# Gates of a hybrid encoder layer by the exponential and VectorE's reciprocal, in place of ScalarE's sigmoid and silu

## Chip, cores and metric

The kernel runs on 1 core of one Trainium2 chip. The metric is the device time of one launch in microseconds. Three runs of the kernel before gave 1577.31 to 1579.09 us, median 1578.4.

## The reference, cut to what matters

One layer over 272 tokens (16 learned ones and 256 of the input), width 2048, float32: RMSNorm, one input projection, a convolution group and a gated DeltaNet group side by side, one output projection, a residual, then RMSNorm and a mixture of 32 experts. The gates that the change touches are these:

```
u = rmsnorm(h, attn_norm[l])
glu_a, glu_b, qkv, z, beta_logit, decay_logit = split_in_proj(u @ w_in[l])
# conformer_conv
y = glu_a * jax.nn.sigmoid(glu_b)
y = causal_depthwise_conv(y, w_dw) + b_dw          # 31 taps
...
# gated_deltanet
qkv = jax.nn.silu(causal_depthwise_conv(qkv, sc_w))   # 4 taps
...
o = chunk_gated_delta_rule(q, k, v, beta, g)
o = o * lax.rsqrt(jnp.mean(o * o, axis=-1, keepdims=True) + EPS) * norm_g
o = o * jax.nn.silu(z)
```

## The kernel before

The input projection makes 48 tiles of 128 output columns by 272 tokens (256 for z), one after the other, in two PSUM banks by turns: bank `n % 2` for tile n. `TILES` fixes their order by kind: "b" and "a" are the halves of the convolution's gate, "c" the 24 tiles of q, k and v, "z" the 8 tiles of the output gate. The order is b b a a b b a a (tiles 0 to 7), 12 c (8 to 19), b b a a (20 to 23), 12 c (24 to 35), b b a a (36 to 39), 8 z (40 to 47). TensorE makes each tile in four quarters (`project`, L704). Before it starts tile n it waits until tile n-2 has been read from the bank (`tile_read0`, `tile_read1`).

Each engine has its instructions in a fixed order written out by hand. Between the quarters TensorE makes steps of the delta rule (`delta`): six groups, one for each half of the heads and each chunk of tokens (one chunk of 16, two of 128). The steps of a group are "turn" (transposes), "decay", "lvl0" (L750 and the lines behind it), then pairs a and b of a triangular solve (L773 and L790, L793; L769 and L786 for the last), "solve" (L799), "apply" (L808, L810), "back" (L817). `STEP_SLOTS` says behind which quarter a step comes. ScalarE, VectorE and GpSimd make their parts of a step in the same order, each between its own work on tiles. ScalarE's part has Ln and Exp for the norms (L1249 to L1258, L1281, L1283) and copies of the solve's products (L1266, L1268, L1271). VectorE's part of "lvl0" is L1568 to L1575, of the solve L1582 to L1590. GpSimd makes the masks (L1996).

ScalarE's work on a tile of kind b is a sigmoid from the bank into `gate_e`, of kind z a silu from the bank into `gate_e` (both in L1295); that read frees the bank. `gate_e` has two halves, used by turns. For a c tile it copies the bank to `raw` (L1206), which frees the bank; VectorE convolves (L1529, L1531), and ScalarE applies silu to the tile before (L1211). ScalarE's functions lie in table sets: `use_table` loads a set (L1160) only when the name differs from the last one, and its calls stand ahead of the waits. VectorE's work on an a tile is one product of bank and gate (L1663), which frees the bank; on a z tile two products or copies of `gate_e` into `mixT` (L1674, L1676), and the bank is long free. All VectorE's gaps are filled with the taps of the 31-tap convolution (L1635), two behind each quarter once the delta steps run.

After tile 47 the output projection (L852) takes banks 0 and 1 first: it waits until both have been read 24 times, then for the last "back" step. Layer norm, router, gather and experts follow. SyncE issues all weight loads; those of the experts wait for slots that the output projection frees (L542), and later for the experts' own products.

Of the kernel before, what the change touches and what calls it, by code (L numbers as in the profile page):

```python
# [207 lines left out]
def hybrid_kernel(nc, x, meta, attn_norm, w_in, conv_dw_w, conv_dw_b, conv_ln_g, conv_ln_b, short_conv_w,  # L208
                  a_log, dt_bias, delta_norm_g, w_out, ffn_norm, w_group, b_group, w_router, b_router,
                  w_gate, w_up, w_down, final_norm, cst_in, masks_in, out):  # L210
    with ExitStack() as ctx:
# [3 lines left out]
        def sem(name):  # L215
            return ctx.enter_context(nc.semaphore(name))
# [158 lines left out]
        tile_read1 = sem("tile_read1")  # L375
        short_done = sem("short_done")
        silu_done = sem("silu_done")
        gated = sem("gated")
        conv_tap = sem("conv_tap")
        delta_pe = sem("delta_pe")  # L380
# [769 lines left out]
        def _(act):  # L1150
            act_fn = nc.scalar.activation
            own = Order(act, order_act)

            table = ""

            def use_table(name):

                nonlocal table
                if name != table:
                    act.preload_act_table_set(name)  # L1160
                table = name

            def ln_exp_table():
                use_table("natural_log_exp_and_others")
            ln_exp_table()

            def rstd_of(i, m):
# [45 lines left out]

            def gate_logits():

                ln_exp_table()
                act.wait_ge(gate_dve, 2)
                act_fn(tb[:, :, :], ta[:, :, :], ACT.Exp, scale=-1.0).then_inc(gate_act, 1)
                act_fn(beta[:, :, :], ba_tok[:, :, 0:NH], ACT.Exp, scale=-1.0).then_inc(gate_act, 1)
                act.wait_ge(later_loaded, 16 * N_LATER)  # L1220
                act_fn(ea, alog_b[:, :], ACT.Exp).then_inc(gate_act, 1)
                act.wait_ge(gate_act, 1)
                act_fn(ta[:, :, :], tb[:, :, :], ACT.Ln, bias=1.0).then_inc(gate_act, 1)

            def decays():

                ln_exp_table()
                act.wait_ge(gsum_done, 1)
                for c, (_, m) in enumerate(CHUNKS):
                    for at, n_ in ((0, m), (8, m), (16, P)):  # L1230
                        act_fn(egs[0:n_, c, at:at + 8], banks[6][0:n_, 24 * c + at:24 * c + at + 8], ACT.Exp
                               ).then_inc(gexp_ready, 1)

            def delta():
                for g in GROUPS:
                    c, hh = g
                    t0, m = CHUNKS[c]
                    act.wait_ge(delta_pe, PE_AT[(g, "turn")])
                    act_fn(k_tok[0:m], bk[2][0:m], ACT.Copy)
                    act_fn(r_tok[0:m], bk[3][0:m], ACT.Copy)  # L1240
                    last = act_fn(scratch[0:m], bk[2][0:m], ACT.Square)
                    if c:
                        last = act_fn(x_inv[0:m], bk[4][0:m], ACT.Square)
                    last.then_inc(delta_act, 1)
                    yield

                    ln_exp_table()
                    act.wait_ge(delta_dve, DVE_AT[(g, "turn")])
                    own.then(act_fn(lnt[0:m], kk[0:m], ACT.Ln, bias=EPS))  # L1249
                    if c:  # L1250
                        own.then(act_fn(lnq[0:m], qq[0:m], ACT.Ln, bias=EPS))
                    own.settle()
                    own.then(act_fn(rk[0:m], lnt[0:m], ACT.Exp, scale=-0.5))
                    if c:
                        own.then(act_fn(rq[0:m], lnq[0:m], ACT.Exp, scale=-0.5))
                        own.then(act_fn(rq2[0:m], lnq[0:m], ACT.Exp, scale=-1.0))
                    act.wait_ge(delta_pe, PE_AT[(g, "decay")])
                    act_fn(decay[0:m, :, 0:m], bk[6][0:m, :, 0:m], ACT.Exp).then_inc(delta_act, 1)  # L1258
                    if c:
                        act_fn(att[0:m, :, 0:m], bk[7][0:m, :, 0:m], ACT.Exp).then_inc(delta_act, 1)  # L1260
                    yield
                    yield
                    for v in range(1, n_levels(c)):
                        act.wait_ge(delta_pe, PE_AT[(g, f"a{v}")])
                        if c == 0:
                            last = act_fn(scratch[0:m, :, 0:m], bk[3][0:m, :, 0:m], ACT.Copy)  # L1266
                        elif v == JOIN:
                            last = act_fn(scratch[0:CAP, :, CAP:P], bk[3][0:CAP, :, CAP:P], ACT.Copy)  # L1268
                        else:
                            for b_, lo in zip(A_BANKS, HALVES):  # L1270
                                last = act_fn(scratch[lo, :, lo], bk[b_][lo, :, lo], ACT.Copy)  # L1271
                        last.then_inc(delta_act, 1)
                        yield
                        yield
                    act.wait_ge(delta_pe, PE_AT[(g, "solve")])
                    act_fn(w_tok[0:m], bk[7][0:m], ACT.Copy).then_inc(delta_act, 1)
                    yield
                    if c:
                        ln_exp_table()
                        act.wait_ge(delta_dve, DVE_AT[(g, "apply")])  # L1280
                        own.then(act_fn(lnt[0:m], oo[0:m], ACT.Ln, bias=EPS))  # L1281
                        own.settle()
                        act_fn(ro[0:m], lnt[0:m], ACT.Exp, scale=-0.5).then_inc(delta_act, 1)  # L1283
                    yield
                    if c:
                        yield

            def gate(n, kind, m):

                use_table("silu_and_others" if kind == "z" else "sigmoid_and_others")  # L1290
                act.wait_ge(tile_done, n + 1)
                if m >= 2:
                    act.wait_ge(gated, m - 1)
                width = SEQ if kind == "z" else T
                return act_fn(gate_e[:, T * (m % 2):T * (m % 2) + width], banks[n % 2][:, 0:width],  # L1295
                              ACT.Silu if kind == "z" else ACT.Sigmoid)

            steps = delta()
            i_c = m_gate = 0
            for n, (kind, j, _, _) in enumerate(TILES):  # L1300
                for _ in range(sum(STEP_SLOTS[n])):
                    next(steps, None)
                if kind == "c":
                    use_table("silu_and_others")
                    take_raw(n, i_c)

                    if i_c % (QKV // 2) > 0:
                        silu_raw(i_c - 1)
                    if n in LAST_C:
                        silu_raw(i_c)  # L1310
                    i_c += 1
                elif kind in "bz":

                    gate(n, kind, m_gate).then_inc((tile_read0, tile_read1)[n % 2], 1)
                    m_gate += 1
                if n == 12:
                    gate_logits()
                if n == 15:
                    decays()
# [1 line left out]
                pass  # L1321


            ln_exp_table()
            for i in range(4):
                act.wait_ge(ln_dve, i + 1)
                act_fn(ln_sq[i], mixT[:, 2 * i:2 * i + 2, :], ACT.Square).then_inc(ln_act, 1)
            for i in range(4):
# [2 lines left out]
                                scale=1.0 / P))  # L1331
                own.settle()
                act_fn(ln_sq[i], ln_sq[i], ACT.Exp, scale=-0.5).then_inc(ln_act, 1)
            use_table("silu_and_others")
            for i in range(4):
                act.wait_ge(ln_dve, 5 + i)
                act_fn(mixT[:, 2 * i:2 * i + 2, :], mixT[:, 2 * i:2 * i + 2, :], ACT.Silu).then_inc(mix_done, 1)  # L1337
# [75 lines left out]
                pair(r * PAIRS + PAIRS - 1, True)  # L1413


            use_table("silu_and_others")
            act.wait_ge(plan_ready, 1)
            silu(0, 0)
            pair(0, False)
# [31 lines left out]
        def _(dve):  # L1451
# [3 lines left out]
            def step(ins):  # L1455

                own.then(ins)
                own.settle()
# [195 lines left out]
            def gate(n, kind, j, m):  # L1654

                nonlocal n_gated, n_silu_z
                width = SEQ if kind == "z" else T
                e = gate_e[:, T * (m % 2):T * (m % 2) + width]
                if kind == "a":

                    dve.wait_ge((tile_read0, tile_read1)[n % 2], n // 2)
                    dve.wait_ge(tile_done, n + 1)
                    step(tt(glu[:, j, HISTORY:], banks[n % 2][:, 0:T], e, ALU.mult))  # L1663
                    n_gated = j + 1
                    dve.sem_inc((tile_read0, tile_read1)[n % 2], 1)
                else:
                    dve.wait_ge((tile_read0, tile_read1)[n % 2], n // 2 + 1)
                    for c in (1, 2):
                        v, ec = mixT[:, 8 + j, P * (c - 1):P * c], e[:, P * (c - 1):P * c]
                        g = (c, j // 4)  # L1670
                        if g in back_done:

                            dve.wait_ge(delta_dve, DVE_AT[(g, "back")])
                            own.then(tt(v, v, ec, ALU.mult))  # L1674
                        else:
                            own.then(dve.tensor_copy(v, ec))  # L1676
                    own.settle()
                    n_silu_z += 1

                dve.sem_inc(gated, 1)  # L1680

            steps = delta()
# [354 lines left out]
```

## Time and profile before

| | us |
|---|---|
| median of 3 runs | 1578.4 |
| the profiled execution, its own time | 1579.09 |
| its span, first to last instruction | 1577.3 |
| TensorE busy | 1540.8 |
| VectorE busy | 524.0 |
| ScalarE busy | 229.9 |
| of it 36 table loads | 46.2 |
| mean granted TensorE clock | 0.994 |

The span is what the trace covers; the time of the execution holds some 2 us more. Busy time of an engine is no measure of its limit: waits are read from the lists of waits and the timelines.

### The profile page before, as it was taken

How to read it: one execution, taken by the hardware profiler on the slowest of the kernel's cores; microseconds unless marked ns; L12 is line 12 of the kernel's file. 1: busy time of each engine (PE TensorE's matmuls, PEld its weight loads, DVE VectorE, ACT ScalarE, POOL GpSimd, SP SyncE). 2: the span in 40 equal slices, each digit the busy share in tenths (PEclk: the TensorE clock that was granted, in tenths of full speed). 3: DMA queues.
4: the chain of work that ended last, by engine and by line, in shares of the span. 5: the costliest groups of instructions: out<-in, count | busy, mean ns of one | idle time of the engine just before them, and what ended most of it. 6: DMA issues, size and time to landing. Idle time of an engine off the chain costs nothing.

```text
span 1577.3 us, 19577 instructions
## 1 busy us (share of the span) xinstructions
PE 1540.8 (98%) x8083; PEld 842.0 (53%) x8083; DVE 524.0 (33%) x1110; ACT 229.9 (15%) x481; POOL 52.9 (3%) x57
## 2 busy tenths in 40 slices
PE   8999999999999999999999999999999999999997
PEld 6878777777776445444344344344434434434432
DVE  2466237843484213222221221321221321321323
ACT  2002223132221303100000100100000000000003
POOL 0000021102020000000000000000000000000000
PEclk9999999999999999999999999999999999999999
DMA  9634231232234126899999999999999999999995
GB/s 346 201 128 168 107 108 38 71 107 107 108 108 189 77 107 267 354 371 429 427 429 428 429 428 428 429 428 429 428 430 428 429 428 429 429 428 430 427 429 201
DMA packets 69575, 479.50 MB, mean 304 GB/s; under 512 B 11506, under 2 KB 20227, under 8 KB 41987
## 3 DMA queue, kind: packets, MB, share of 16 engines
q1 hardware_dynamic: 69232, 478.55, 74.0%
q8 instruction: 37, 0.61, 0.2%
q10 hardware_dynamic: 290, 0.23, 0.1%
q14 instruction: 16, 0.12, 0.0%
HBM read 476.66 MB, written 2.10 MB: 304 GB/s over the span
## 4 chain that ended last, share of the span: by engine, by line
PE 71%; DMA 22%; DVE 4%; SPq 1%; issue 1%; ACT 1%; ACTq 0%; POOL 0%; DVEq 0%
DMA ring<-in_w_up_dram 21%; PE bank L704 20%; PE bank L1030 18%; PE bank L1053 9%; PE bank L1100 7%; PE bank L852 7%; PE bank L995 1%; DVE region_m L1635 1%; PE bank L790 1%; PE bank L1046 1%; PE bank L773 1%; SPq L568 1%; PE bank L793 0%; PE bank L667 0%; DMA rows<-in_conv_ln_b_dram 0%
## 5 line engine op out<-in xcount | busy, mean ns | idle before, releaser
L1030 PE MATMUL bank<-ring,region_m 128*64 128x512 f32 x2048 | 456.3, 596 | 7.9 <-DMA ring<-in_w_up_dram 7.9
L704 PE MATMUL bank<-region_u,ring 128*128 128x272 f32 (+1 forms) x1536 | 373.8, 396 | 0.0
L704 PEld LDWEIGHTS bank<-region_u,ring 128*128 128x128 f32 x1536 | 284.6, 190 | 55.1 <-issue 0.9
L1030 PEld LDWEIGHTS bank<-ring,region_m 128*64 128x64 f32 x2048 | 141.6, 137 | 283.5 <-issue 261.8
L1053 PE MATMUL bank<-region_qy,region_s 128*64 128x512 f32 x992 | 218.2, 592 | 0.5 <-issue 0.5
L1053 PEld LDWEIGHTS bank<-region_qy,region_s 128*64 128x64 f32 x992 | 72.2, 137 | 140.7 <-issue 140.4
L1869 DVE TENSOR_TENSOR region_s<-region_s,bank 64x512 f32<-64x512 f32 x32 | 22.1, 692 | 348.4 <-ACT region_s L1378 348.4
L995 PEld LDWEIGHTS bank<-region_m,region_u 128*128 128x128 f32 x960 | 108.4, 192 | 12.2 <-issue 12.2
L1100 PE MATMUL bank<-region_m 128*128 128x512 f32 x256 | 114.8, 600 | 0.0
L1885 DVE TENSOR_TENSOR region_h<-region_h,bank 128x512 f32<-128x512 f32 x128 | 88.0, 688 | 79.1 <-PE bank L1100 79.1
L1635 DVE SCALAR_TENSOR_TENSOR region_m<-region_qy,cols,region_m 128x256 f32<-128x256 f32 x240 | 110.6, 525 | 2.1 <-DVE region_qy L1663 1.0
L995 PE MATMUL bank<-region_m,region_u 128*128 128x128 f32 x960 | 111.2, 277 | 0.0
L1879 DVE COPY region_m<-bank 64x512 f32<-64x512 f32 x64 | 44.1, 689 | 169.8 <-PE bank L1053 169.3
L852 PE MATMUL bank<-ring,region_m 128*128 128x512 f32 x192 | 85.0, 595 | 0.8 <-ACT region_m L1337 0.8
L1100 PEld LDWEIGHTS bank<-region_m 128*128 128x128 f32 x256 | 46.9, 190 | 67.6 <-issue 63.7
L1383 ACT ACTIVATE region_s<-bank 128x256 f32<-128x256 f32 x32 | 12.3, 384 | 431.8 <-PE bank L1046 431.7
L1396 ACT ACTIVATE region_m<-bank 64x512 f32<-64x512 f32 x64 | 37.9, 592 | 195.9 <-PE bank L1053 195.5
L1861 DVE TENSOR_TENSOR region_m<-bank,g_ffn_pm 128x512 f32<-128x512 f32 x64 | 44.1, 692 | 56.9 <-PE bank L995 56.7
L852 PEld LDWEIGHTS bank<-ring,region_m 128*128 128x128 f32 x192 | 35.8, 190 | 43.5 <-issue 43.4
L1378 ACT ACTIVATE region_s<-bank 64x512 f32<-64x512 f32 x32 | 18.9, 589 | 226.2 <-PE bank L1030 226.2
L1160 ACT ACT_TABLE_LOAD x36 | 46.2, 1283 | 1.4 <-PEq L2026 0.8
L2011 POOL TENSOR_TENSOR region_u<-region_h,ring 128x512 f32<-128x512 f32 x2 | 3.0, 1496 | 1093.2 <-DVE region_h L1885 1093.2
(263 smaller groups left out, 843.8 us busy)
## 6 DMA issues: line engine op xcount, KB each, us to landing
ring<-in_w_gate_dram SPq DMA_DIRECT2D x63, 2048.0 KB, 12.2
ring<-in_w_up_dram SPq DMA_DIRECT2D x63, 2048.0 KB, 16.7
region_qy<-in_w_down_dram SPq DMA_DIRECT2D x62, 2048.0 KB, 15.6
ring<-in_w_in_dram SPq DMA_DIRECT2D x40, 1024.0 KB, 7.4
ring<-in_w_out_dram SPq DMA_DIRECT2D x12, 1024.0 KB, 5.5
ring<-in_w_in_dram SPq DMA_DIRECT2D x16, 512.0 KB, 5.4
region_qy<-in_w_out_dram SPq DMA_DIRECT2D x4, 1024.0 KB, 13.1
ring<-in_w_down_dram SPq DMA_DIRECT2D x2, 2048.0 KB, 26.4
```

Of the source, the lines that this page charges most:

```text
L704: last = mm(banks[n % 2][:, 0:width], slot[s][:, 512 * k + P * j:512 * k + P * (j + 1)], uT[:, 4 * g + k, T - width:T], start=g == k == 0, ...
L852: last = mm(banks[4 * t + q], mixT[:, k, P * t:P * (t + 1)], w_slots[n_k][:, BANK * q:BANK * (q + 1)], start=n_k == 0, stop=n_k == KD - 1)
L995: last = mm(banks[5 + g % 2][:, P * k:P * (k + 1)], un[:, t, c0:c0 + P], sel_g[:, t, :], start=t == 0, stop=t == TT - 1)
L1030: last = mm(banks[x_][CAP * v:CAP * (v + 1), :], uTe[:, 4 * g + k, CAP * x_:CAP * (x_ + 1)], w_gu[v][:, k0:k0 + 512], start=g == k == 0, s ...
L1053: last = mm(banks[3 + q][CAP * v:CAP * (v + 1), :], hidT[:, x_, f, :], w[f // 2][:, c0:c0 + BANK], start=n_f == 0, stop=n_f == KF - 1)
L1100: mm(banks[sb[i % len(sb)]], sel_wT[:, P * (i // 4):P * (i // 4 + 1)], ypair[:, column(i)], start=True, stop=True).then_inc(scatter_done, 1)
L1160: act.preload_act_table_set(name)
L1396: last = act_fn(ypair[CAP * x_:CAP * (x_ + 1), c0:c0 + BANK], banks[4][CAP * v:CAP * (v + 1), :], ACT.Copy)
L1635: stt(out=acc, in0=glu[:, j, tap:tap + SEQ], scalar=dw_w[:, tap, j:j + 1], in1=acc if tap else cols[:, 33 + j:34 + j].to_broadcast([P, SEQ ...
L1861: tt(uTe[:, 4 * g:4 * g + 4, :], bk[GATHER_FIRST[g] if isinstance(p, int) and p == 0 else 5 + g % 2], b4(g_ffn_pm[:, 4 * g:4 * g + 4]), AL ...
L1879: last = dve.tensor_copy(ypair[CAP * x_:CAP * (x_ + 1), c0:c0 + BANK], banks[3][CAP * v:CAP * (v + 1), :])
L1885: tt(v, v, banks[sb[i % len(sb)]][:, :], ALU.add).then_inc(scatter_read, 1)
```

## The change

ScalarE makes `exp(-x)` of every b and z tile. VectorE adds 1 and takes the reciprocal. For an a tile it then multiplies with the bank as before. For a z tile it multiplies the bank with the result, so that the silu is made, and then does what it did before. The signal that a z bank has been read moves from ScalarE to the end of VectorE's work, and a new semaphore `gate_exp` tells VectorE that the exponential is there. In `gate` the two instructions on an a tile stand behind both waits, that for the tile of the gate's other half too. Exp and Ln share one table set. `use_table` goes: `ln_exp_table` now always loads the log/exp set, and is called at the start, behind the silus of a c tile, and ahead of the second norm and the last one. No line loads the silu set any more; the compiler places a load of it before a silu where it isn't there. In the part before layer norm, ScalarE's order is otherwise the same.

```
-            def use_table(name):
-                nonlocal table
-                if name != table:
-                    act.preload_act_table_set(name)
-                table = name
...
             def ln_exp_table():
-                use_table("natural_log_exp_and_others")
+
+                act.preload_act_table_set("natural_log_exp_and_others")
...
             def gate(n, kind, m):
-                use_table("silu_and_others" if kind == "z" else "sigmoid_and_others")
                 act.wait_ge(tile_done, n + 1)
...
-                return act_fn(gate_e[:, T * (m % 2):T * (m % 2) + width], banks[n % 2][:, 0:width],
-                              ACT.Silu if kind == "z" else ACT.Sigmoid)
+                return act_fn(gate_e[:, T * (m % 2):T * (m % 2) + width], banks[n % 2][:, 0:width], ACT.Exp, scale=-1.0)
...
                 if kind == "c":
-                    use_table("silu_and_others")
                     take_raw(n, i_c)
 
                     if i_c % (QKV // 2) > 0:
                         silu_raw(i_c - 1)
                     if n in LAST_C:
                         silu_raw(i_c)
+                    if i_c % (QKV // 2) > 0:
+                        ln_exp_table()
                     i_c += 1
-                elif kind in "bz":
+                elif kind == "z":
+                    gate(n, kind, m_gate).then_inc(gate_exp, 1)
+                    m_gate += 1
+                elif kind == "b":
...
# VectorE
                 e = gate_e[:, T * (m % 2):T * (m % 2) + width]
-                if kind == "a":
+                if kind == "z":
+                    dve.wait_ge(gate_exp, j + 1)
+                else:
 
                     dve.wait_ge((tile_read0, tile_read1)[n % 2], n // 2)
                     dve.wait_ge(tile_done, n + 1)
+                step(ts(e, e, 1.0, None, ALU.add))
+                step(dve.reciprocal(e, e))
+                if kind == "a":
                     step(tt(glu[:, j, HISTORY:], banks[n % 2][:, 0:T], e, ALU.mult))
                     n_gated = j + 1
-                    dve.sem_inc((tile_read0, tile_read1)[n % 2], 1)
                 else:
-                    dve.wait_ge((tile_read0, tile_read1)[n % 2], n // 2 + 1)
+                    step(tt(e, banks[n % 2][:, 0:SEQ], e, ALU.mult))
                     for c in (1, 2):
...
                     n_silu_z += 1
 
+                dve.sem_inc((tile_read0, tile_read1)[n % 2], 1)
                 dve.sem_inc(gated, 1)
```

The calls of `ln_exp_table` in `gate_logits`, `decays`, in the delta steps and before the layer norm's Square go, and the two calls of `use_table("silu_and_others")` before the layer norm's silu and before the experts.

## Rows read from the trace of the kernel before

**Rows 1.** The page: busy time with instructions, and the chain's shares by engine.
```profile
PE 1540.8 (98%) x8083; PEld 842.0 (53%) x8083; DVE 524.0 (33%) x1110; ACT 229.9 (15%) x481; POOL 52.9 (3%) x57
...
PE 71%; DMA 22%; DVE 4%; SPq 1%; issue 1%; ACT 1%; ACTq 0%; POOL 0%; DVEq 0%
```
**Rows 2.** Waits of TensorE, 40 to 620 us: total, times, longest.
```profile
PE bank L773 <- DVE region_h L1575: 5.8, 4, 3.1
PE bank L817 <- DVE region_h L1607: 2.2, 4, 1.0
```
**Rows 3.** Groups by line: busy us and mean ns; idle time before them.
```profile
L1160 ACT ACT_TABLE_LOAD x36 | 46.2, 1283 | 1.4 <-PEq L2026 0.8
...
L1529 DVE TENSOR_SCALAR region_m<-region_qy,cols 128x272 f32<-128x272 f32 x24 | 8.7, 361 | 19.2 <-ACT region_qy L1206 19.2
L1663 DVE TENSOR_TENSOR region_qy<-bank,region_m 128x272 f32<-128x272 f32 x8 | 3.5, 442 | 38.2 <-PE bank L704 38.1
L1765 DVE RECIPROCAL small<-small 128x1 f32<-128x1 f32 x2 | 0.3, 164 | 0.1
L1519 DVE RECIPROCAL small<-small 128x24 f32<-128x24 f32 x1 | 0.3, 302 | 0.0
```
**Rows 4.** Timelines of ScalarE, GpSimd, TensorE, first short group: start, length, [idle].
```profile
166.32 1.28 ACT L1160 ACT_TABLE_LOAD   x1
167.61 0.20 ACT L1249 ACTIVATE small<-small 16x4 f32<-16x4 f32 x1
...
168.98 0.31 POOL L1996 TENSOR_TENSOR region_s<-region_h,masks 16x64 f32<-16x64 f32 x1 [2.68 <-DVE region_h L1561]
...
169.63 0.26 PE L750 MATMUL bank<-cst,region_s 16*16 16x16 f32 x4
```
**Rows 5.** Timeline of ScalarE behind a c tile.
```profile
309.71 0.38 ACT L1268 ACTIVATE region_h<-bank 64x256 f32<-64x256 f32 x1 [2.99 <-PE bank L769]
```
**Rows 6.** Timeline of VectorE from tile 42 to the layer norm.
```profile
448.95 0.48 DVE L1674 TENSOR_TENSOR region_m<-region_m 128x128 f32<-128x128 f32 x2
449.58 0.69 DVE L1568 TENSOR_TENSOR region_h<-cst,bank 128x512 f32<-128x512 f32 x1 [0.15 <-DVE region_m L1674]
...
463.31 0.85 DVE L1588 TENSOR_TENSOR region_h<-region_h,bank 64x256 f32<-64x256 f32 x2 [0.45 <-PE bank L793]
464.18 0.85 DVE L1590 TENSOR_TENSOR region_h<-region_h,bank 64x256 f32<-64x256 f32 x2
...
474.49 0.85 DVE L1588 TENSOR_TENSOR region_h<-region_h,bank 64x256 f32<-64x256 f32 x2 [1.05 <-PE bank L793]
...
485.13 0.41 DVE L1585 TENSOR_TENSOR region_h<-region_h,bank 64x256 f32<-64x256 f32 x1 [1.59 <-PE bank L786]
...
498.91 0.49 DVE L1674 TENSOR_TENSOR region_m<-region_m 128x128 f32<-128x128 f32 x2
513.08 0.69 DVE L1713 SCALAR_TENSOR_TENSOR region_m<-bank,region_m 128x512 f32<-128x512 f32 x1 [13.68 <-PE bank L915]
```
**Rows 7.** Timeline of TensorE in the z tiles.
```profile
453.55 0.68 PE L773 MATMUL bank<-region_h,region_m 64*64 64x64 f32 x16 [2.07 <-DVE region_h L1575]
...
465.17 0.68 PE L773 MATMUL bank<-region_h,region_m 64*64 64x64 f32 x16
...
486.85 1.05 PE L799 MATMUL bank<-region_h 128*128 128x128 f32 x8
...
498.29 13.90 PE L852 MATMUL bank<-ring,region_m 128*128 128x512 f32 x32
```
**Rows 8.** Timeline of TensorE behind the longest wait.
```profile
278.81 3.53 PE L704 MATMUL bank<-region_u,ring 128*128 128x272 f32 x8
...
283.55 2.10 PE L704 MATMUL bank<-region_u,ring 128*128 128x272 f32 x8
```
**Rows 9.** Busy time by stretch, each engine; then granted clock, DMA share, GB/s.
```profile
280.00:282.40 2.40, 2.40 (x8) 1.35 (x8) 2.40 (x4) 0.02 (x1) 0.99 (x1) 0.50 0.36 117
...
440.00:480.00 40.00, 37.20 (x368) 30.06 (x366) 32.38 (x62) 7.69 (x17) 10.60 (x8) 1.00 0.31 107
```

More of the change, by code:

```diff
@@ L377, in hybrid_kernel @@
         silu_done = sem("silu_done")
+        gate_exp = sem("gate_exp")
         gated = sem("gated")
@@ L1152, in _ @@
             own = Order(act, order_act)
-            table = ""
-            def use_table(name):
-                nonlocal table
-                if name != table:
-                    act.preload_act_table_set(name)
-                table = name
             def ln_exp_table():
-                use_table("natural_log_exp_and_others")
+                act.preload_act_table_set("natural_log_exp_and_others")
             ln_exp_table()
@@ L1214, in gate_logits @@
             def gate_logits():
-                ln_exp_table()
                 act.wait_ge(gate_dve, 2)
@@ L1225, in decays @@
             def decays():
-                ln_exp_table()
                 act.wait_ge(gsum_done, 1)
@@ L1245, in delta @@
                     yield
-                    ln_exp_table()
                     act.wait_ge(delta_dve, DVE_AT[(g, "turn")])
@@ L1278, in delta @@
                     if c:
-                        ln_exp_table()
                         act.wait_ge(delta_dve, DVE_AT[(g, "apply")])
@@ L1321, in _ @@
                 pass
-            ln_exp_table()
             for i in range(4):
@@ L1333, in _ @@
                 act_fn(ln_sq[i], ln_sq[i], ACT.Exp, scale=-0.5).then_inc(ln_act, 1)
-            use_table("silu_and_others")
             for i in range(4):
@@ L1413, in one_round @@
                 pair(r * PAIRS + PAIRS - 1, True)
-            use_table("silu_and_others")
             act.wait_ge(plan_ready, 1)
```

## The prediction

> **What bounds the kernel now.** I read the page first: TensorE is busy for 1540.8 of 1577.3 us, and the chain that ended last is 71% TensorE and 22% DMA [rows 1]. So the time moves only where TensorE comes to wait, or where the expert weights start to stream later. The change touches the mixer (up to tile 47, about 498 us). The first expert loads wait for slots that the output projection frees (L542 in SyncE's order, L852 in TensorE's). These loads have no other anchor, so a microsecond that TensorE loses before 498 us delays the output projection, then the weight stream, then the end: I carry it over one to one.
>
> Next the waits of TensorE over the mixer. The largest is L773 behind VectorE's L1575, 5.8 us in 4 times [rows 2]: the first product of the triangular solve waits for VectorE. None of its waits in the recurrence is put down to ScalarE. ScalarE's 36 table loads take 46.2 us [rows 3], but beside a TensorE that doesn't wait for them. Then I read the timelines of all engines where the recurrence runs beside the projections.
>
> **The change, part by part.** *Gates on ScalarE.* The sigmoid of 8 tiles and the silu of 8 become 16 exponentials of the same shapes: no change in length. Their table loads go. Where they were, TensorE waited for VectorE or for nothing, so I take 0 for this gain. Its bounds are 0 and 2.2 us, the wait at L817, whose release passes through ScalarE [rows 2].
>
> *Table loads at the 22 silus of convolved tiles.* Silu is not in the log/exp set, so each of the 22 needs one load ahead of it, and the new line loads the log/exp set behind it. That puts two loads between the copy of a tile (L1206) and ScalarE's next step of the recurrence. A load takes 1283 ns [rows 3], and in the timeline the next instruction starts some 0.02 us behind it, so the two take 2.6 us and the lost overlap of copy and silu 0.1: 2.7 us. The tightest place at 128 tokens is L1268, where ScalarE had been idle for 2.99 us [rows 5]: it still fits. (The Trainium skill, "ScalarE: Activation LUTs", What ACT_TABLE_LOAD costs, gives about 2.66 us for every switch, 1.38 of it a drain. This trace doesn't agree: the load before the Ln of [rows 4] starts at 166.32 and the Ln at 167.61, 1.29 us apart. By the page the pair would take 5.3 us, not 2.6.)
>
> It does not fit in the first group of each half, of 16 tokens. There the order of ScalarE before is silu, load, Ln; after, load, silu, load, Ln. The Ln (L1249) starts at 167.61, right behind its load; with one more load ahead, it starts 1.3 to 1.4 us later. GpSimd's mask at 168.98 hangs on it through VectorE and ends at 169.29; TensorE's L750 starts at 169.63 [rows 4]. So TensorE waits 169.29 + 1.4 - 169.63 = 1.1 us, and again in the second half (the same rows come again 177 us later): **+2.2 us**. Bounds: 0 and 2.8.
>
> *Gates on VectorE.* Each "a" tile gets an add of 1 and a reciprocal, each "z" tile these and one product that reads the bank. The add: the scaling of L1529, 128x272, takes 361 ns [rows 3]; I take 0.36. The product: L1663 takes 442 ns [rows 3]; for 256 columns 0.42. The reciprocal has no row of this size. The two that there are take 164 ns for one column and 302 ns for 24 [rows 3], 6.0 ns a column, so 164 + 255 x 6.0 = 1694 ns for 256. Lower bound: the rate of the product, 0.42. Upper: all of the 302 ns by column, 12.6 ns each, 3.2 us. I take 1.69, since it is the slope of the operation itself. With three settles of about 0.04 us, **D = 2.6 us** more for each z gate (1.3 to 4.1), and 2.2 for each a gate. (The Trainium skill, "VectorE: DVE Perf Modes", First, the fixed hardware budget, says that a reciprocal repeats its divide step 8 times. Taken as 8 cycles of 0.96 GHz, 8.3 ns a column, it would make D 3.2 and the sum below about 16 instead of 12. The two rows lie nearer to 6.)
>
> The a gates are covered: VectorE's idle time behind tiles 38 and 39 is of the size of the 2.2 us or above it, and in the early tiles only taps follow. The z gates stand in VectorE's queue ahead of the recurrence, whose results TensorE waits for. Going through them:
>
> Tiles 40 and 41: idle time of VectorE behind them covers it.
>
> Tile 42: the gate starts at 448.95, and the solve's preparation follows with no gap [rows 6]. Its end already keeps TensorE waiting: L773 at 453.55, 2.07 us [rows 7]. All of D shows: **+2.6**.
>
> Tile 43: behind it L1588 had 0.45 us idle; L1590 ends 465.03, and L773 takes its result at 465.17 [rows 6, 7], 0.14 spare: 2.6 - 0.59 = **+2.0**.
>
> Tile 44: idle 1.05 us at L1588 of 474.49 [rows 6], 0.14 spare again: **+1.4**.
>
> Tile 45: idle 1.59 us at L1585 [rows 6]; the 1.0 us left lies within the time until L799 at 486.85 [rows 7]: 0.
>
> Tiles 46 and 47: here the bank's release counts. Before, ScalarE let go of the bank with its own read; now VectorE does, behind its four or five instructions. VectorE has no gap around these two. The last gate (L1674) starts at 498.91 and ends 499.40 [rows 6]; with its own D and that of tile 46, 504.6. TensorE begins the output projection at 498.29 [rows 7] with the four chunks of bank 0, 8 of the 32 instructions that take 13.90 us, so 3.5 us, and needs the other bank at 501.8: **+2.8**.
>
> The taps are not late for the layer norm: VectorE is idle 13.68 us before it [rows 6].
>
> *TensorE's clock.* After the longest wait, 3.1 us at L773 in the first half [rows 2], the granted clock is 0.50 in the stretch from 280 us on (1.2 GHz, where 1.00 is 2.4) [rows 9], and 8 projection instructions take 3.53 us where the next 8 take 2.10 [rows 8]. After the wait of 2.07 at 453.55 there is no such fall. The wait grows to 4.7 us, so I expect the fall there: about 1.5, of which VectorE's lateness covers a little: **+1.2**. At the last wait of 2.8 us it may come or not; I leave it out of the sum and in the range.
>
> Sum: 2.2 + 2.6 + 2.0 + 1.4 + 2.8 + 1.2 = 12.2 us. The profiled execution took 1579.1 us, 0.7 over the median of 1578.4 us: 1591.3 by the one, 1590.6 by the other. I say **1591 us**.
>
> **The rivals.** *The reciprocal is cheap* (D about 1.3, VectorE at one column a cycle). Then tile 42 gives 1.3, tile 43 0.7, tile 44 0.2, the last bank 499.4 + 2.6 - 501.8 = 0.2; with clock and the short groups 1.2 + 2.2: 5.8 us, **1584 us**. For it: nothing but the small sizes of the two rows; against it their slope.
>
> *VectorE becomes the bound of the z tiles.* From 440 to 480 us it is busy for 32.4 of 40 us [rows 9], and four gates add 10.4. If its reciprocal takes the upper bound (D 4.1), tile 42 gives 4.1, 43 3.5, 44 2.9, 45 some 1.2, the banks 5.8, two clock falls 2.7, short groups 2.2: 22 us, **1600 us**. For it: the little time left in that stretch. Against it: the slope again.
>
> *The table switches held the recurrence, and their removal gives back more than the gates cost* (the other side). It would decide if ScalarE's loads stood behind TensorE's waits at L773 and L817: 5.8 + 2.2 = 8.0 us less [rows 2], and D hidden: **1570 us**. Against it: L773's wait ends in L1575, which follows L1568 at 449.58, whose idle time is put down to VectorE's own gate [rows 6].
>
> *A table switch holds ScalarE longer than the load's row.* If each cost twice its 1.3 us, the pair at L1268 overruns 2.99 us by 2.3; the copies of the solve behind three convolved tiles of the second group would come late by more than the 2.0 us of cover that one projection quarter gives, some 1.3 us each, and the short groups would cost 2.5 more in all: 12 + 4 + 3 = 19 us, **1598 us**. Against it: the 1.29 us above.
>
> *The cost is hidden* (the a and z gates in idle time, short groups late by less than their spare time): **1579 us**. It needs D under about 1 us, since tile 42 has no spare time at all.
>
> **How the numbers follow.** Within 0.2% (3.2 us) is what a measurement here can't tell from no change. The forecast, +8 to +17 us, gets 0.68; the cheap reciprocal 0.16; VectorE as the bound 0.04; longer switches 0.02; hidden 0.07; the faster side 0.03. So slower 0.90, same 0.07, faster 0.03. The range leaves out the last two and the far end: 1583 to 1598 us; the likeliest case alone is 1587 to 1596.
>
> **What would show it.** In the profile after: reciprocals of 256 columns near 1.7 us; 49 table loads instead of 36 and ScalarE 17 us busier; VectorE about 37 us busier; TensorE waiting about 4.7 us at L773 of tile 43 with a clock of 0.5 behind it; a wait for VectorE at the second quarter of the first output chunks; a wait of 1 us at L750 of the short groups; the expert stage unchanged in length but later. The prediction is wrong if the reciprocal is off its slope, if the wait instruction of a silu runs before its table load so that convolved tiles come late, or if the expert stage takes up the delay.

## The result and the profile after

The changed kernel takes 1591.4 us (median of 4 runs, 1591.1 to 1592.4), the kernel before beside it 1578.1: ratio 1.0085, 95% interval 1.0067 to 1.0102. So it is slower by 13.3 us, where the forecast's sum was 12.2. The profiled execution took 1592.06 us with a span of 1590.1. TensorE's lines are one higher than before. VectorE's are twelve lower from the 4-tap convolution to the taps (L1575 is now L1563), eight in the last products of a z gate (L1674 is now L1666), and seven in the product of an a gate and from the layer norm on.

The page after: busy times and the chain, against [rows 1].

```profile
PE 1544.2 (97%) x8083; PEld 843.1 (53%) x8083; DVE 558.3 (35%) x1150; ACT 248.2 (16%) x494; POOL 52.9 (3%) x57
...
PE 71%; DMA 20%; DVE 6%; ACT 1%; issue 1%; SPq 1%; POOL 0%; ACTq 0%; DVEq 0%
```

VectorE is busy 34 us longer and ScalarE 18. Neither is the bound by its share; what counts is that VectorE's part of the chain went from 4% to 6% of the span. The waits of TensorE from 40 to 640 us say where (total, times, longest):

```profile
PE bank L774 <- DVE region_h L1563: 8.5, 4, 4.7
PE bank L853 <- DVEq L1672: 2.7, 1, 2.7
PE bank L751 <- POOL region_s L1989: 2.4, 3, 1.1
PE bank L774 <- DVE region_h L1578: 2.4, 3, 1.1
```

Against [rows 2] the wait behind L1563 (L1575 before) has grown by 2.7 us, and three are new or longer: L853 for VectorE's release of a bank (L1672 is the signal's line), L751 for GpSimd's mask (0.3 us in all before), L774 for the solve's step (0.8 us in all before). The wait at L818 (L817 before) is 2.2 us in all, as it was.

The groups of the new operations, by shape (busy us and mean ns), against [rows 3]:

```profile
L1654 DVE RECIPROCAL region_m<-region_m 128x272 f32<-128x272 f32 x8 | 14.8, 1853 | 0.3
L1654 DVE RECIPROCAL region_m<-region_m 128x256 f32<-128x256 f32 x8 | 14.0, 1753 | 0.3
...
L1659 DVE TENSOR_TENSOR region_m<-bank,region_m 128x256 f32<-128x256 f32 x8 | 3.4, 424 | 0.3
...
L1653 DVE TENSOR_SCALAR region_m<-region_m 128x256 f32<-128x256 f32 x8 | 2.3, 284 | 0.0
```

A reciprocal of 256 columns takes 1753 ns; the two shapes differ by 100 ns for 16 columns, 6.25 ns a column.

ScalarE behind the first tile of a short group, GpSimd and TensorE, by their timelines (start, length, idle before), against [rows 4]:

```profile
164.90 0.40 ACT L1199 ACTIVATE region_qy<-bank 128x272 f32<-128x272 f32 x1 [0.49 <-PE bank L705]
165.32 1.28 ACT L1204 ACT_TABLE_LOAD   x1
166.61 0.43 ACT L1204 ACTIVATE region_qy<-region_m 128x272 f32<-128x272 f32 x1
167.06 1.28 ACT L1157 ACT_TABLE_LOAD   x1
168.35 0.20 ACT L1239 ACTIVATE small<-small 16x4 f32<-16x4 f32 x1
...
169.73 0.31 POOL L1989 TENSOR_TENSOR region_s<-region_h,masks 16x64 f32<-16x64 f32 x1 [4.11 <-DVE region_h L1549]
...
170.09 0.26 PE L751 MATMUL bank<-cst,region_s 16*16 16x16 f32 x4 [1.07 <-POOL region_s L1989]
```

Two loads stand around the silu where one stood behind it, the Ln comes late, the mask with it, and L751 waits 1.07 us. Behind a c tile the same two loads just fit: 0.29 us of idle time are left before the next copy, where 3.02 stood in the kernel before.

```profile
295.17 1.28 ACT L1204 ACT_TABLE_LOAD   x1
296.47 0.43 ACT L1204 ACTIVATE region_qy<-region_m 128x272 f32<-128x272 f32 x1
296.92 1.28 ACT L1157 ACT_TABLE_LOAD   x1
298.49 0.77 ACT L1261 ACTIVATE region_h<-bank 64x256 f32<-64x256 f32 x2 [0.29 <-PE bank L774]
```

VectorE from the gate of tile 42 on, against [rows 6]:

```profile
450.32 0.28 DVE L1653 TENSOR_SCALAR region_m<-region_m 128x256 f32<-128x256 f32 x1
450.63 1.75 DVE L1654 RECIPROCAL region_m<-region_m 128x256 f32<-128x256 f32 x1
452.42 0.42 DVE L1659 TENSOR_TENSOR region_m<-bank,region_m 128x256 f32<-128x256 f32 x1
452.88 0.49 DVE L1666 TENSOR_TENSOR region_m<-region_m 128x128 f32<-128x128 f32 x2
453.63 0.69 DVE L1556 TENSOR_TENSOR region_h<-cst,bank 128x512 f32<-128x512 f32 x1 [0.26 <-DVE region_m L1666]
```

And TensorE, against [rows 7]:

```profile
457.59 1.12 PE L774 MATMUL bank<-region_h,region_m 64*64 64x64 f32 x16 [4.75 <-DVE region_h L1563]
458.64 3.78 PE L705 MATMUL bank<-region_u,ring 128*128 128x256 f32 x8
...
472.20 0.68 PE L774 MATMUL bank<-region_h,region_m 64*64 64x64 f32 x16 [1.05 <-DVE region_h L1578]
...
484.39 0.68 PE L774 MATMUL bank<-region_h,region_m 64*64 64x64 f32 x16 [0.98 <-DVE region_h L1578]
...
506.33 3.60 PE L853 MATMUL bank<-ring,region_m 128*128 128x512 f32 x8
512.63 12.26 PE L853 MATMUL bank<-ring,region_m 128*128 128x512 f32 x24 [2.70 <-DVEq L1672]
```

The output projection starts at 506.33 where it started at 498.29, 8.0 us later. Its first chunk of 8 runs, then 2.70 us of wait for the bank of tile 47, and the 24 others take 12.26 us, where all 32 took 13.90. At half clock they lose some 1.8 us more. The stretches (busy time of each engine, then granted clock, DMA share, GB/s) show both falls, behind the wait of 4.75 and behind that of 2.70:

```profile
458.00:462.00 4.00, 4.00 (x22) 3.04 (x18) 3.84 (x5) 0.76 (x2) 2.37 (x2) 0.50 0.06 25
...
514.00:517.00 3.00, 3.00 (x5) 1.29 (x4) 0.00 (x0) 0.00 (x0) 0.00 (x0) 0.50 1.00 423
```

The rest is carried over whole. By the chain the last eight products of the scatter start at 1574.15; in the kernel before they started at 1561.73. That is 12.4 us of the 12.8 by which the spans differ.

### The profile page after: what moved, and what is told of

The parts are those of the page before. It is cut to its first block, busy times and chain, and to the rows that moved or that the text cites. A ratio compares the mean times of both kernels' runs of the same rounds, so it can differ in the third digit from the quotient of the medians.

```text
span 1590.1 us, 19638 instructions
## 1 busy us (share of the span) xinstructions
PE 1544.2 (97%) x8083; PEld 843.1 (53%) x8083; DVE 558.3 (35%) x1150; ACT 248.2 (16%) x494; POOL 52.9 (3%) x57
## 4 chain that ended last, share of the span: by engine, by line
PE 71%; DMA 20%; DVE 6%; ACT 1%; issue 1%; SPq 1%; POOL 0%; ACTq 0%; DVEq 0%
DMA ring<-in_w_up_dram 19%; PE bank L1031 19%; PE bank L705 18%; PE bank L1054 9%; PE bank L1101 7%; PE bank L853 7%; PE bank L996 2%; DVE region_m L1623 1%; PE bank L1047 1%; PE bank L774 1%; PE bank L791 1%; DVE region_m L1654 1%; SPq L569 1%; PE bank L668 0%; PE bank L794 0%
## 5 line engine op out<-in xcount | busy, mean ns | idle before, releaser
L705 PE MATMUL bank<-region_u,ring 128*128 128x272 f32 (+1 forms) x1536 | 375.2, 397 | 0.0
L705 PEld LDWEIGHTS bank<-region_u,ring 128*128 128x128 f32 x1536 | 285.6, 191 | 55.5 <-issue 0.9
L996 PEld LDWEIGHTS bank<-region_m,region_u 128*128 128x128 f32 x960 | 108.4, 192 | 12.2 <-issue 12.2
L853 PE MATMUL bank<-ring,region_m 128*128 128x512 f32 x192 | 87.0, 605 | 3.5 <-DVEq L1672 2.7
L853 PEld LDWEIGHTS bank<-ring,region_m 128*128 128x128 f32 x192 | 36.3, 193 | 47.7 <-issue 44.1
L1519 DVE SCALAR_TENSOR_TENSOR region_m<-region_qy,cols,region_m 128x272 f32<-128x272 f32 x72 | 37.4, 519 | 2.6
## 6 DMA issues: line engine op xcount, KB each, us to landing
ring<-in_w_gate_dram SPq DMA_DIRECT2D x63, 2048.0 KB, 12.2
```

The source lines that it names most:

```text
L705: last = mm(banks[n % 2][:, 0:width], slot[s][:, 512 * k + P * j:512 * k + P * (j + 1)], uT[:, 4 * g + k, T - width:T], start=g == k == 0, ...
L853: last = mm(banks[4 * t + q], mixT[:, k, P * t:P * (t + 1)], w_slots[n_k][:, BANK * q:BANK * (q + 1)], start=n_k == 0, stop=n_k == KD - 1)
L996: last = mm(banks[5 + g % 2][:, P * k:P * (k + 1)], un[:, t, c0:c0 + P], sel_g[:, t, :], start=t == 0, stop=t == TT - 1)
L1519: ins = stt(out=acc, in0=raw[:, ch, j:j + T], scalar=short_w[:, j, ch:ch + 1], in1=acc, op0=ALU.mult, op1=ALU.add)
```

## The experiments

Each experiment is compared with the kernel before, run beside it on the same chip (median 1578.3 to 1578.4). Where one is set against the changed kernel, that is the 1591.4 us of the section above, whose own kernel before took 1578.1. The edits are shown shortened to their meaning.

**One part alone, three times.** First only the table loads: gates as before, in the c tiles

```
-                    use_table("silu_and_others")
                     take_raw(n, i_c)
                     if i_c % (QKV // 2) > 0:
+                        use_table("silu_and_others")
                         silu_raw(i_c - 1)
                     ...
+                    if i_c % (QKV // 2) > 0:
+                        ln_exp_table()
```

> The kernel before with one part of the change alone: the loads of the silu set and of the log/exp set around the silus of the convolved tiles, gates as before. Theory (three separate costs): 1.07 us of wait at the lvl0 step (L750) of each of the two groups of 16 tokens and nothing else, so +2.1 us over before. Rival (the table loads are the main cost and ScalarE is late for the solve's copies too): +6 us or more, with waits of TensorE put down to ScalarE.

Measured: 1580.1 us (10 runs), ratio 1.0009 (1.0000 to 1.0019), +1.7 us. TensorE's waits have one row that has grown, L750's (0.3 us in one wait before), and none that is new:

```profile
PE bank L773 <- DVE region_h L1577: 5.8, 4, 3.1
PE bank L750 <- POOL region_s L1998: 2.4, 3, 1.1
```

There are 65 table loads in this kernel, 29 more than before (the gates' own loads are still there): 37 us more of ScalarE for some 2 us of time. The rival, with ScalarE late for the solve, is out.

Second the b and a gates alone:

```
-                use_table("sigmoid_and_others")      # kind b
+                ln_exp_table()
-                ... ACT.Sigmoid)
+                ... ACT.Exp, scale=-1.0)
# VectorE, kind a
+                    step(ts(e, e, 1.0, None, ALU.add))
+                    step(dve.reciprocal(e, e))
                     step(tt(glu[:, j, HISTORY:], banks[n % 2][:, 0:T], e, ALU.mult))
```

> The kernel before with the b and a gates alone by exponential and reciprocal (8 of 16), tables otherwise loaded as before. Theory: VectorE's 2.2 us more for each a tile lie in its idle time, 0 us, within 1 us of before. Rival (each of VectorE's microseconds counts): 8 x 2.2 = up to +17 us.

Measured: 1578.0 us (10 runs), ratio 0.9998 (0.9988 to 1.0007), -0.3 us: nothing that can be told from 0. TensorE's waits are those of the kernel before, row by row. Half of the reciprocals cost no time.

Third the z gates alone, with the bank's release on VectorE:

```
-                ... ACT.Silu, then_inc(tile_read)    # ScalarE, kind z
+                ... ACT.Exp, scale=-1.0, then_inc(gate_exp)
# VectorE, kind z
+                    dve.wait_ge(gate_exp, j + 1)
+                    step(ts(e, e, 1.0, None, ALU.add))
+                    step(dve.reciprocal(e, e))
+                    step(tt(e, banks[n % 2][:, 0:SEQ], e, ALU.mult))
                     ...
+                    dve.sem_inc((tile_read0, tile_read1)[n % 2], 1)
```

> The kernel before with the z gates alone by exponential and reciprocal on VectorE, which also frees the bank; tables otherwise as before. Theory: 2.65 at tile 42, 1.1 and 1.0 at tiles 43 and 44, 2.7 for the last bank, and two stretches of TensorE at half clock of 1.9 each: +11.3 us. Rival (the parts cost only together, since ScalarE's loads also hold the exponentials): +5 us or less.

Measured: 1588.1 us (4 runs), ratio 1.0059 (1.0042 to 1.0076), +9.8 us; 11.3 lies within the interval (6.6 to 12.0). Its waits are those of the changed kernel without L751's: 4.7 us at L774, 2.4 in three more, 2.7 at L853. The three parts alone give 1.7 - 0.3 + 9.8 = 11.2 us of the 13.3, each of the parts uncertain by 1.5 to 2.7 us to either side: they add up, as far as this can tell.

**The length of VectorE's work, shorter and longer.** The changed kernel with the reciprocal of the z tiles left out:

```
-                step(dve.reciprocal(e, e))
+                if kind == "a":
+                    step(dve.reciprocal(e, e))
```

> The changed kernel with the reciprocal of the z tiles left out (the z gate then multiplies with 1 + exp(-z) and not with its inverse), all other instructions and waits kept. Theory: VectorE's extra per z tile falls from 2.65 to 0.9 us. Tile 42 then costs 0.9, with a wait of 3.0 us at L774, tiles 43 and 44 about 0.3 and 0, the last bank none; the clock falls after the first wait only if 3.0 us are enough (1.9). With the tables' 2.1 that is +3.3 us over before, or +5.2 with the fall. Rival (what costs is that VectorE frees the bank and waits for ScalarE, not the length of its work): +9 us or more.

Measured: 1582.7 us (10 runs), ratio 1.0025 (1.0015 to 1.0035), +4.4 us, between the two figures of the theory and half of the rival's. The wait at tile 42 is 2.96 us as forecast, the waits behind the solve's step are 0.8 us in all as before the change, and the one for the bank is gone. In the profiled execution no half clock follows that wait, which by the theory means +3.3. What is above it stands in the first half: behind the wait of 3.09 us there, half clock lasts longer than in the kernel before (from L774 to the second group of projection products behind it 6.60 us, before 5.35). So no wait is left that the signal on VectorE would be needed to explain, and the length of VectorE's work is what costs. The signal alone, without longer work, was not run.

And with three reciprocals instead of one:

```
                 step(dve.reciprocal(e, e))
+                if kind == "z":
+                    step(dve.reciprocal(e, e))
+                    step(dve.reciprocal(e, e))
```

> The changed kernel with three reciprocals one behind the other instead of one in each z gate (the value is the same): 3.6 us more of VectorE per z tile, D = 6.2. Theory (VectorE's queue is now what paces the z tiles): tiles 40 and 41 lose their cover and show about 2.5 and 3.5, tiles 42 to 45 about 3.6 each, the last bank some 3.6 to 5: +22 to +28 us over the changed kernel. Rival (only the places with no idle time show, tile 42 and the last bank): +8 us.

Measured: 1622.4 us (4 runs), ratio 1.0275 (1.0259 to 1.0291), +44 us over before and 31 over the changed kernel, more than the 22 to 28 of the theory. Its added work is 8 tiles by 3.5 us, 28 in all. The list of waits shows VectorE behind nearly every step of the z tiles:

```profile
PE bank L774 <- DVE region_h L1563: 12.1, 4, 8.3
PE bank L774 <- DVE region_h L1578: 9.5, 3, 4.6
PE bank L853 <- DVEq L1675: 7.9, 2, 4.7
PE bank L818 <- DVE region_h L1595: 4.7, 4, 3.4
PE bank L800 <- DVE region_h L1573: 3.2, 1, 3.2
...
PE bank L741 <- DVE small L1538: 2.0, 1, 2.0
```

All of TensorE's waits together are some 24 us longer than in the changed kernel. That the time grew by 31 goes with a lower granted clock (0.986 over the span, 0.991 in the changed kernel; 0.87 and 0.91 from 440 to 480 us); how much of it the clock took was not measured. Of the 28 us that were added, then, most show as waits, where of the 8 x 2.67 us of the change itself 7.4 did (2.7, 1.05, 0.98 and 2.7).

**Room made in VectorE's queue.** The kernel before, without the change, with no taps between VectorE's decay and lvl0 steps:

```
                         if due:
                             next(steps, None)
+                            n_step += 1
-                        some_taps(TAPS_BETWEEN)
+                        if n_step < 1 or STEPS[n_step - 1] not in HELD:   # decay, groups of 128 tokens
+                            some_taps(TAPS_BETWEEN)
```

> The kernel before, without any part of the change, but VectorE makes no taps of the 31-tap convolution between its decay and lvl0 steps in the groups of 128 tokens; the taps come later. Theory (L773's wait behind L1575 is VectorE's queue, the four taps stretched beside GpSimd's masks): the waits of 3.1 and 2.07 us shrink to under 1 each, the half clock behind the first goes: -5 us, about 1573. Rival (the wait is for GpSimd or for TensorE's own lvl0 products): within 1 us of before.

Measured: 1574.4 us (9 runs), ratio 0.9974 (0.9965 to 0.9984): 3.9 us faster than the kernel before, where 5 were forecast. The waits at L773 behind L1575 have fallen from 5.8 to 2.5 us in all, the longest from 3.1 to 1.2 (not under 1, as forecast), and the clock is 1.00 from 276 to 290 us, where it was 0.88:

```profile
PE bank L773 <- DVE region_h L1575: 2.5, 4, 1.2
```

The same in the changed kernel:

> The changed kernel with the same four taps held back. Theory: the z gate of tile 42 then fits where the taps were; the wait of 4.7 falls to about 2 and that of 3.1 in the first half to under 1, with less half clock: -6 to -9 us against the changed kernel, about 1584, still slower than before. Rival (the z gates cost their length wherever they stand): -4 us, only the first half's part.

Measured: 1583.8 us (10 runs), ratio 1.0032 (1.0022 to 1.0041), 7.6 us under the changed kernel, so more than in the kernel before: the gate of tile 42 has moved into the place of the taps. L774's wait behind L1563 is 3.1 us in all, 1.2 at most, where it was 8.5 and 4.7. The wait for the bank of tile 47 has grown from 2.7 to 3.5 us.

The bank of tile 47 wanted later, by TensorE's order in the changed kernel:

```
             pe.wait_ge(tile_read0, len(TILES) // 2)
             project_out(0, range(4), (0,))
+            pe.wait_ge(delta_dve, DVE_AT[(GROUPS[-1], "back")])
+            project_out(0, range(4), (2, 3))
             pe.wait_ge(tile_read1, len(TILES) // 2)
             project_out(0, range(4), (1,))
-            pe.wait_ge(delta_dve, DVE_AT[(GROUPS[-1], "back")])
-            project_out(0, range(4), (2, 3))
```

> The changed kernel with one edit in TensorE's order: the first four chunks of the output projection go to banks 0, 2, 3 and then 1, so that the bank of tile 47 is wanted 7 us later. Theory (the wait of 2.7 us is for VectorE's release of that bank, and the half clock behind it follows from the wait): -2.7 and -1.9, so -4.6 us against the changed kernel. Rival (the wait moves to the back step or to the layer norm): 0.

Measured: 1587.5 us (4 runs), ratio 1.0055 (1.0040 to 1.0071), 3.9 us under the changed kernel, where 4.6 were forecast. The output projection's first chunks run through in TensorE's timeline, with no wait and no half clock:

```profile
507.30 13.90 PE L853 MATMUL bank<-ring,region_m 128*128 128x512 f32 x32
521.03 3.60 PE L916 MATMUL bank<-region_m,cst 128*128 128x512 f32 x8
```

Both together:

> The changed kernel with both repairs: the four taps held back between decay and lvl0, and the output projection's banks in the order 0, 2, 3, 1. Theory (the two costs are independent): -7.6 and -3.5 with the last stretch of half clock -1.9 in most executions, about 1579, equal to before; what is left of the change is 2.1 for the short groups and some 3 at tiles 43 to 45, and the held taps pay for it. Rival (they share a cost): 1583.

Measured: 1578.8 us (10 runs), ratio 1.0003 (0.9994 to 1.0013). The changed kernel with both repairs takes the time of the kernel before, and is still 4.4 us behind the kernel before with the first repair alone.

**Going on from the held taps.** The kernel before with the held taps, and VectorE's work on tiles 26 and 42 behind the next lvl0 step:

```
-                    gate(n, kind, j, m_gate)
+                    work = lambda n=n, kind=kind, j=j, m=m_gate: gate(n, kind, j, m)
                     ...
+                if work and n_step and STEPS[n_step - 1] in HELD and n > 25:
+                    late.append(work)          # called behind the next step
```

> The kernel before with the four taps held back, and VectorE's work on tiles 26 and 42 (the 4-tap convolution, and the z gate) moved behind its next lvl0 step. Theory: the waits at L773 that are left, 1.2 and 0.7 us, fall to 0.3 each: -1.3 us against the held taps alone, about 1573. Rival (the moved work makes VectorE late at the next step of the solve): 0 or slower.

Measured: 1574.5 us (11 runs), ratio 0.9978 (0.9969 to 0.9987): no gain over the held taps, as the rival had it. The waits show it moved:

```profile
PE bank L773 <- DVE region_h L1590: 3.1, 3, 1.8
...
PE bank L773 <- DVE region_h L1575: 1.5, 4, 0.5
```

Against the held taps alone L1575 gave back 1.0 us and L1590 took 2.1 (from 1.0 to 3.1), one step later. The same on the changed kernel with both repairs:

> The changed kernel with the held taps, the moved work of tiles 26 and 42 and the banks in the order 0, 2, 3, 1. Theory: moving the gate of tile 42 behind lvl0 hands its 2.65 us to the next solve step, where 0.5 us are idle, so most of the cost comes back there: within 1 us of the kernel without the move, 1578 to 1579. Rival (behind lvl0 the gate is free): 1576.

Measured: 1580.3 us (10 runs), ratio 1.0016 (1.0007 to 1.0026), 1.5 us slower than without the move, and more than the 1 us that the theory allowed. The waits moved here too: behind L1563 they fell from 3.1 to 1.5 us, behind the solve's step they rose from 3.1 to 4.9, so their sum is nearly the same. The work has to go somewhere in VectorE's queue, and in front of one step it costs about the wait that it costs in front of another. What the profiled execution lost beside that (it is the slowest of the ten) is clock. Behind a wait of 1.72 us its 8 projection products take 3.66 us, where they take 1.99 without the move:

```profile
458.37 0.68 PE L774 MATMUL bank<-region_h,region_s 64*64 64x64 f32 x16 [1.72 <-DVE region_h L1578]
458.98 3.66 PE L705 MATMUL bank<-region_u,ring 128*128 128x256 f32 x8
```

The mean granted clock of the ten runs is 0.993 to 0.996, that of the ten without the move 0.995 to 0.996, so some of the others lost it too. Three had 0.996 all the same and took 1578.8 to 1580.3 us: the clock is not shown to be all of the 1.5 us.

Nothing in the study is faster than the kernel before with the held taps, 1574.4 us.

## Why the prediction was right

*What bounds the kernel, and one to one.* Right: from the output projection on, the two traces differ by a constant 12.4 to 12.7 us. The DMA stage neither took up the delay nor added to it.

*Gates on ScalarE, 0.* Right: the second experiment has five table loads fewer, those of the b gates, and gains nothing that can be told from 0. The z gates' loads were not taken away alone; the wait at L817, the bound of this gain, stayed at 2.2 us in the changed kernel.

*Table loads of the c tiles, 2.2 us.* Measured 1.07 us of wait in each short group, 2.1; alone 1.7 by the first experiment. The 49 loads are there (25, 22, and one each before the two later silus). At the prediction's tightest place (L1258 now, at 309.97 us) 0.27 us are left of the 2.99, so the pair and the silu took 2.72 where 2.7 were forecast.

*The reciprocal, 1.69 us from a slope of 6.0.* Measured 1.753 and a slope of 6.25 ns. The two rows of 1 and 24 columns were enough to tell it from the rate of a product and from the 8.3 ns a column that the prediction set beside it. D was 2.67 us: from the start of L1653 at 450.32 to that of L1666 at 452.88, and 0.11 us more of settling behind it.

*The a gates, 0.* Right, by the second experiment, whose waits have not moved.

*Tile 42, +2.6.* Measured 4.75 - 2.07 = 2.7. On TensorE this wait stands between the quarters of tile 43, which is how the prediction's list of signs names it.

*Tiles 43 and 44, +2.0 and +1.4.* Mis-sized: 1.05 and 0.98. The direction was right, but a part of the gate itself was stretched before by a mask of GpSimd that ran at the same time, and is not any more. The kernel before shows it at tile 43, in VectorE's line beside that of the mask, and the changed kernel at the same place:

```profile
460.26 1.56 DVE L1674 TENSOR_TENSOR region_m<-region_m 128x128 f32<-128x128 f32 x2
460.34 1.33 POOL L1996 TENSOR_TENSOR region_s<-region_h,masks 128x512 f32<-128x512 f32 x1 [4.01 <-PE bank L773]
```

```profile
466.31 1.33 POOL L1989 TENSOR_TENSOR region_s<-region_h,masks 128x512 f32<-128x512 f32 x1 [5.94 <-PE bank L774]
466.55 1.75 DVE L1654 RECIPROCAL region_m<-region_m 128x256 f32<-128x256 f32 x1
...
468.80 0.49 DVE L1666 TENSOR_TENSOR region_m<-region_m 128x128 f32<-128x128 f32 x2
```

The two products are 1.07 us shorter, since the mask now runs beside the reciprocal, which it does not stretch, and is done before they start: 2.67 - 1.07 less the 0.45 us of idle time is 1.15, near the 1.05. Tile 44 is the same case. There a copy of the gate had been stretched:

```profile
471.65 0.76 DVE L1676 COPY region_m<-region_m 128x128 f32<-128x128 f32 x1
```

It takes 0.22 us in the changed kernel (at 481.26), and 2.67 - 0.54 less the 1.05 us of idle time is 1.08, near the 0.98. The 0.14 us that the prediction counted as spare are none: they stand between VectorE's end and TensorE's start in the changed kernel too (L1578 ends at 472.06, L774 starts at 472.20). I had set all of D against the idle time, and not asked what else moves when the gate does.

*Tile 45, 0, and the last bank, +2.8.* Right: no wait, and 2.70 us. The eighth experiment takes it away.

*TensorE's clock, +1.2.* This is the weak term. The fall came where it was forecast, but was larger. From L774 at tile 42 to the next one it is 7.96 us, where the kernel before took 6.03 with 0.42 of wait in it. So half clock took 2.35 us, not 1.5, the wait that it covered gave 0.4 back, and 1.9 remain. And the second fall, which I left out of the sum, cost 2.0 (12.7 us late behind it, less 8.0 and 2.7). That makes 3.9 us instead of 1.2. Two things hide it in the total: the steps of tiles 43 and 44, too large by 1.4 us, and the part before the input projection, in which this execution happened to be 0.7 us ahead of the other (L705 starts at 20.34 us, L704 at 21.03): 2.1 + 2.7 + 1.9 + 1.05 + 1.0 + 2.7 + 2.0 - 0.7 = 12.75, against 12.8 by the spans. So the nearness of the total is in part luck.

*The rivals.* The cheap reciprocal is out by its row. VectorE as the bound of the z tiles is not what happens at D = 2.67; at the D of 6.2 of the fifth experiment it is, where 3.5 us more per tile cost 31 us. From which D on it holds was not looked for. The longer table switch is out by the two loads that fit in 2.99 us. The faster side is out by the second experiment and by the waits at L774 and L818, none of which has shrunk. *Hidden* is out as well: the two repairs bring the time back to that of the kernel before, but 4.4 us of cost are left against the kernel before with the same taps held.

## What to carry to other kernels

Moving work from an engine that is 15% busy to one that is 33% busy says nothing yet: look at what stands behind it in the receiver's queue, and who waits for that. Here the eight a gates cost nothing, and of the eight z gates four places cost all (tiles 42, 43, 44 and the last bank), by the idle time of the receiving engine just behind each. Where a wait already ends at the receiving engine, what is added in front of it shows in full (2.7 us of 2.67 at tile 42, 0.9 of 0.9 without the reciprocal), and taking filler work out from in front of it pays without any change of the arithmetic. When a signal that frees a buffer moves to another engine, follow it to the last use of the buffer, where no further tile covers it.

## What the runs showed of the hardware

Between 1.7 and 3 us, whether the granted clock falls behind a wait of TensorE is not told by the wait's length. At the same place, tile 42's L773 (L774), the table-load experiment waited 2.06 us and had half clock behind it, in the stretch from 455 to 458 us; the kernel before waited 2.07 and had none; the experiment without reciprocals waited 2.96 and had none. The last experiment had half clock behind 1.72 us, one step later. The rows of the first and the third of these, each from some 1 to 2 us behind its wait:

```profile
455.00:458.00 3.00, 3.00 (x20) 1.99 (x21) 2.67 (x5) 0.38 (x1) 1.20 (x1) 0.54 0.59 249
```

```profile
458.00:462.00 4.00, 4.00 (x46) 3.32 (x45) 3.97 (x8) 0.74 (x2) 1.65 (x2) 1.00 0.59 195
```

In these traces a wait of some 2 to 3 us was followed by nothing more or by up to some 2 us more. It differs by execution too: the ten runs of the table-load experiment took 1578.96 to 1582.08 us, the fastest at a mean granted clock of 0.996 and the slowest at 0.993. What decides the fall stays open.

Some of VectorE's work from SBUF to SBUF is stretched beside GpSimd's masks, and that is large enough to shift a forecast: two products of 128 columns took 1.56 us beside a mask and 0.49 without, a copy of 128 columns 0.76 and 0.22. The reciprocal is not: it takes 1.75 us beside a mask as elsewhere. (The Trainium skill, "SBUF — State Buffer", section "SBUF: two separate sides", says that the port pair which the two engines share is an exclusive lock for the whole instruction, and that a VectorE instruction with two inputs in SBUF takes part in it. The rows of the two products agree with it, though no run here was made to test it.)
